# Three input norms of a hybrid encoder: their deviations spread over partitions through a row in DRAM instead of on TensorE

## The reference, cut to what matters

```
h = rmsnorm(x, norm_w[layer, 0]);  m = mixer(h);     x = x + rmsnorm(m, norm_w[layer, 1])
h = rmsnorm(x, norm_w[layer, 2]);  f = conv_ffn(h);  x = x + rmsnorm(f, norm_w[layer, 3])
rmsnorm(x, w) = x * rsqrt(mean(x*x, axis=-1) + eps) * w
```

## Time and profile before

| | |
|---|---|
| median of 3 runs | 1341.23 us (1339.83 to 1341.42) |
| the profiled execution, its own time | 1341.43 us |
| span of its trace | 1339.6 us |
| PE busy | 1320.0 us, 99% of the span |
| DVE, ACT, POOL busy | 777.4, 641.8, 621.8 us |
| data moved by DMA | 119.78 MB |

### The profile page before, as it was taken

One profiled execution on the slowest core, in us unless ns is written; L12 is line 12 of the kernel. 1 busy time (PEld: TensorE's weight loads), 2 busy tenths in 40 slices (PEclk: granted clock), 3 DMA queues, 4 the chain that ended last, 5 costly groups with the idle time before them and its releaser, 6 DMA issues.

```text
span 1339.6 us, 16496 instructions
## 1 busy us (share of the span) xinstructions
PE 1320.0 (99%) x6630; PEld 1119.0 (84%) x6630; DVE 777.4 (58%) x890; ACT 641.8 (48%) x1033; POOL 621.8 (46%) x294
## 2 busy tenths in 40 slices
PE   7999999999999999999999999999999999999997
PEld 6878878888898888888889888898998888888887
DVE  5857386840079998885002753386279988882002
ACT  5654787653355444443233576454554544443221
POOL 3344561245424644445553364554535544445551
PEclk9999999999999999999999999999999999999999
DMA  6332111123223332333333223301323333333331
GB/s 206 95 113 85 51 37 40 63 79 98 92 85 103 97 95 94 94 93 100 94 94 103 96 79 95 95 16 63 112 95 95 95 94 98 102 93 88 100 87 63
DMA packets 41452, 119.78 MB, mean 89 GB/s; under 512 B 4384, under 2 KB 12960, under 8 KB 41376
## 3 DMA queue, kind: packets, MB, share of 16 engines
q1 hardware_dynamic: 40160, 116.34, 28.5%
q10 hardware_dynamic: 1216, 2.38, 0.6%
HBM read 116.35 MB, written 2.23 MB: 89 GB/s over the span
## 4 chain that ended last, share of the span: by engine, by line
PE 93%; DVE 4%; ACT 1%; issue 1%; DMA 0%; ACTq 0%; DVEq 0%
PE bank L336 26%; PE bank L337 26%; PE bank L338 26%; PE bank L1774 1%; PE bank L1775 1%; PE bank L1773 1%; PE bank L2077 1%; PE bank L2059 1%; PE bank L1506 1%; PE bank L1509 1%; PE bank L1325 1%; PE bank L387 1%; PE bank L1292 1%; PE bank L1536 1%; DVE sqacc L663 1%
## 5 line engine op out<-in xcount | busy, mean ns | idle before, releaser
L319 POOL TENSOR_TENSOR wlo<-raw,whi 128x1024 fp32r<-128x1024 f32 (+2 forms) x215 | 531.1, 2483 | 633.9 <-ACT whi L313 633.8
L336 PE MATMUL bank<-xw_hi,whi 128*128 128x512 f32 (+1 forms) x1280 | 478.0, 373 | 8.6 <-DVE xw_lo L646 8.1
L338 PE MATMUL bank<-xw_hi,wlo 128*128 128x512 f32 (+1 forms) x1280 | 473.8, 370 | 0.0
L337 PE MATMUL bank<-xw_lo,whi 128*128 128x512 f32 (+1 forms) x1280 | 473.7, 370 | 0.0
L313 ACT ACTIVATE whi<-raw 128x1024 fp32r<-128x1024 f32 (+2 forms) x217 | 221.5, 1025 | 208.0 <-DMA raw<-in_fout 112.2
L336 PEld LDWEIGHTS bank<-xw_hi,whi 128*128 128x128 f32 x1280 | 242.5, 189 | 50.3 <-issue 8.9
L338 PEld LDWEIGHTS bank<-xw_hi,wlo 128*128 128x128 f32 x1280 | 242.3, 189 | 41.1
L337 PEld LDWEIGHTS bank<-xw_lo,whi 128*128 128x128 f32 x1280 | 242.5, 189 | 39.8 <-issue 0.2
L596 DVE RECIPROCAL small<-small 128x2 f32<-128x2 f32 x8 | 1.3, 165 | 315.1 <-ACT small L521 313.7
L715 DVE SCALAR_TENSOR_TENSOR cbuf<-ubuf,par,cbuf 128x510 f32<-128x510 f32 x100 | 168.7, 1687 | 3.5
L711 DVE SCALAR_TENSOR_TENSOR cbuf<-ubuf,par,cbuf 128x510 f32<-128x510 f32 x100 | 144.6, 1446 | 4.7 <-ACT cbuf L844 4.1
(11 more groups left out here) (278 smaller groups left out, 1453.9 us busy)
## 6 DMA issues: line engine op xcount, KB each, us to landing
raw<-in_fin SPq DMA_DIRECT2D x88, 512.0 KB, 3.6
raw<-in_fout SPq DMA_DIRECT2D x32, 448.0 KB, 3.3
raw<-in_gin SPq DMA_DIRECT2D x25, 512.0 KB, 3.6
raw<-in_hin SPq DMA_DIRECT2D x24, 512.0 KB, 3.7
raw<-in_hout SPq DMA_DIRECT2D x16, 512.0 KB, 3.6
raw<-in_fout SPq DMA_DIRECT2D x16, 512.0 KB, 3.6
raw<-in_gout SPq DMA_DIRECT2D x8, 512.0 KB, 3.9
xres<-in_x SPq DMA_DIRECT2D x8, 256.0 KB, 5.8
```

Source lines behind the costliest of these rows:

```text
L319: engine.tensor_tensor(wlo[s][:, 0:n], raw[s][:, 0:n], whi[s][:, 0:n].bitcast(F32), ALU.subtract).then_inc(w_lo, 1)
L336: first = nc.tensor.matmul(out_ap, wh, ah, start=start, stop=False)
L337: nc.tensor.matmul(out_ap, wh, al, start=False, stop=False)
L338: return first, nc.tensor.matmul(out_ap, wl, ah, start=False, stop=stop)
```

## The change

For norms k = 0, 1 and 2, `pe_res_spread` is no longer called. ACT waits for DVE's reciprocal and issues a DMA that stores `small[:, 12:16]` to a row of 512 values in DRAM (token order, so the 512 values are 4 bytes each, apart from each other on the side of DRAM or of SBUF); it then does the weight splits that it did before, waits until the store has landed, and issues a second DMA that loads this row on all 128 partitions of `rstd`. DVE waits for that load. Norm k = -1 stays as it was.

In `gin`, bank 6 is no longer taken by the spread. Blocks 5 and 6 (and every second later pair, 17 and 18 and so on) swap banks 5 and 6, and the waits that name evictions are renumbered.

Semaphores are merged: the three loads for the GLA stage share one, for which DVE waits ahead of the gate weights; `cst` and `rope` share one, for which every reader of `cst` waits; so do the eight stores of the output, and two steps of POOL at the end.

```diff
+        rstd_row = nc.dram_tensor("rstd_row", (1, T), F32).ap()
         def act_res_rstd(act, k, at):
             act.wait_ge(sem("res_ss"), of("res_ss", k) + 1)
             nc.scalar.activation(small[:, 12:16], bank[7][:, 4:8], ACT.Sqrt, bias=prm("eps"),
                                  scale=1.0 / D).then_inc(sem("res_sd"), 1)
+            if k >= 0:
+                act.wait_ge(sem("res_rs"), of("res_rs", k) + 1)
+                act.dma_start(rstd_row[0].rearrange("(b p) -> p b", p=P), small[:, 12:16],
+                              allow_slow_non_contiguous=True).then_inc(sem("rstd_out"), 16)
             his(act, at)
             if k in (0, 2):
                 his(act, at + 1)
+            if k >= 0:
+                act.wait_ge(sem("rstd_out"), 16 * (k + 1))
+                act.dma_start(rstd[:], rstd_row.broadcast_to([P, T])).then_inc(sem("rstd_in"), 16)
+                return
             act.wait_ge(sem("res_sp"), of("res_sp", k) + 1)
             nc.scalar.activation(rstd[:], bank[6][:], ACT.Copy).then_inc(sem("res_rstd"), 1)
...
         def dve_gate_weights(dve):
-            dve.wait_ge(sem("wgk_in"), 16)
+            dve.wait_ge(sem("gla_in"), 48)
...
-            dve.wait_ge(sem("res_rstd"), of("res_rstd", k) + 1)
+            if k < 0:
+                dve.wait_ge(sem("res_rstd"), 1)
+            else:
+                dve.wait_ge(sem("rstd_in"), 16 * (k + 1))
...
         def pe_fin(pe, l):
-                        beside={2: lambda: pe_res_sums(pe, k), 7: lambda: pe_res_spread(pe, k)} if j == g else None)
+                        beside={2: lambda: pe_res_sums(pe, k)} if j == g else None)
...
         def gbank(j):
-            return bank[(2, 3, 5)[j] if j < 3 else (0, 1, 5, 6)[(j - 3) % 4]]
+            return bank[(2, 3, 5)[j] if j < 3 else (0, 1, 6, 5)[(j - 3) % 4]]
...
         def pe_gin(pe):
                 elif j >= V0 + KD:
-                    pe.wait_ge(sem("vtok_dve" if (j - V0) % 2 else "vtok_act"), (j - V0 - KD) // 2 + 2)
+                    pe.wait_ge(sem("vtok_dve" if j in (V0 + KD, V0 + KD + 3) else "vtok_act"), (j - V0 - KD) // 2 + 2)
                 elif j >= 5:
-                    pe.wait_ge(sem("gin_u"), {5: 3, 6: 1}.get(j, j - 3))
+                    pe.wait_ge(sem("gin_u"), {5: 1, 6: 3}.get(j, j - 3))
                 product(pe, base + j, gbank(j)[:], xw_hi, xw_lo,
-                        beside={6: lambda: pe_res_sums(pe, 1), 8: lambda: pe_res_spread(pe, 1)} if j == 3 else None)
+                        beside={6: lambda: pe_res_sums(pe, 1)} if j == 3 else None)
...
                     if i == 0 and g == 0 and b >= 2:
-                        pe.wait_ge(sem("gin_u"), 4 + b)
+                        pe.wait_ge(sem("gin_u"), 9 - b)
...
-            dve.wait_ge(sem("gmask_in"), 16)
-            dve.wait_ge(sem("tri_in"), 16)
...
-            sp.wait_ge(sem("out_stored"), (NREQ * PAIRS - 1) * 16)
-            sp.wait_ge(sem("last_stored"), 16)
+            sp.wait_ge(sem("out_stored"), NREQ * PAIRS * 16)
```

More of the change, by code:

```diff
@@ L819, in pe_hin @@
                     pe.wait_ge(sem("ident_in"), 16)
-                    pe.wait_ge(sem("cst_in"), 16)
+                    pe.wait_ge(sem("cst_in"), 32)
                 block(j)
@@ L921, in dve_hin @@
             turns(dve, SIDE, Z0, conv)
-            dve.wait_ge(sem("cst_in"), 16)
+            dve.wait_ge(sem("cst_in"), 32)
             dve.wait_ge(sem("ident_in"), 16)
@@ L1054, in act_picks @@
             act.wait_ge(sem("ident_in"), 16)
-            act.wait_ge(sem("cst_in"), 16)
+            act.wait_ge(sem("cst_in"), 32)
             for h in (slice(0, 64), slice(64, 128)):
@@ L1397, in dve_mla_rotated @@
         def dve_mla_rotated(dve):
-            dve.wait_ge(sem("rope_in"), 16)
             dve.wait_ge(sem("mla_kr"), 1)
@@ L1790, in act_gla_loads @@
             act.wait_ge(sem("out_m"), of("out_m", 2))
-            act.dma_start(wgk[:], w_gk).then_inc(sem("wgk_in"), 16)
-            act.dma_start(gmask[:], glac[:, 0:T + CH]).then_inc(sem("gmask_in"), 16)
-            act.dma_start(tri[:], glac[:, T + CH:T + CH + 2 * P]).then_inc(sem("tri_in"), 16)
+            act.dma_start(wgk[:], w_gk).then_inc(sem("gla_in"), 16)
+            act.dma_start(gmask[:], glac[:, 0:T + CH]).then_inc(sem("gla_in"), 16)
+            act.dma_start(tri[:], glac[:, T + CH:T + CH + 2 * P]).then_inc(sem("gla_in"), 16)
         def act_gin(act):
@@ L2331, in _ @@
             act.dma_start(cst[:], consts[:, P:NCONST]).then_inc(sem("cst_in"), 16)
-            act.dma_start(cosin[:], rope).then_inc(sem("rope_in"), 16)
+            act.dma_start(cosin[:], rope).then_inc(sem("cst_in"), 16)
             act_hin(act)
@@ L2348, in _ @@
             nc.scalar.activation(rstd[:, 0:SEQ], bank[5][:, 0:SEQ], ACT.Copy).then_inc(sem("last_rstd"), 1)
-            act.wait_ge(sem("last_x"), 1)
-            act.dma_start(ckr(out, KD - 2, 1, 2), ckr(xres, KD - 2, 1, 2)).then_inc(sem("last_stored"), 16)
+            act.wait_ge(sem("last_x"), 2)
+            act.dma_start(ckr(out, KD - 2, 1, 2), ckr(xres, KD - 2, 1, 2)).then_inc(sem("out_stored"), 16)
         @block.gpsimd
@@ L2369, in _ @@
             nc.gpsimd.tensor_tensor(m, m, rstd[:, 0:SEQ].unsqueeze(1).broadcast_to([P, 2, SEQ]), ALU.mult).then_inc(
-                sem("last_t"), 1)
-            pool.wait_ge(sem("last_t"), 1)
+                sem("last_x"), 1)
+            pool.wait_ge(sem("last_x"), 1)
             nc.gpsimd.tensor_tensor(x, x, m, ALU.add).then_inc(sem("last_x"), 1)
```

## The result

The changed kernel takes 1368.64 us (median of 4 runs, 1367.40 to 1370.35) against 1341.33 us (4 runs, 1339.83 to 1341.78): the ratio is 1.0206, 95% interval 1.0193 to 1.0219. It is 27.3 us slower. The forecast was 1341.9 us, and its range ended at 1346.5.

What follows compares the result with a forecast made beforehand. PE's list was taken to bound the kernel: -2.43 us (three spreads) + 3.1 (wait at gate(0)) + 0 + 0 = +0.7 us, giving 1341.9 us against the median of 1341.23; range 1339.0 to 1346.5.

Steps and rivals of the forecast that it cites:

- PE's list: On PE, three spreads of 0.81 us each leave its work: -2.43 us.
- The two thresholds: PE waits at block 6 of the FFNs from C = 8.4 us on (none expected), at gate(0) C - 3.77 (3.1 us).
- C: Time from the end of DVE's reciprocal through store and load to DVE's start: 6.85 us for k = 1, 8.05 for others.
- The store: ACT's DMA of 512 4-byte pieces to DRAM: 4.0 us for k = 1, 4.6 for others, bounds 2.2 and 7.1.
- The rival of the slow store: Store of 4-byte pieces takes 7.1 us, PE waits at gate(0) and both FFNs: +8.1 us, 1349.3; 1 in 4.
- The load: DMA of the row onto 128 partitions: 2.7 us for k = 1, 3.3 for k = 0 and 2.
- The clock: Rival: PE's clock falls in the wait at gate(0), costing 2.4 us more, 1344.3 in all; 1 in 12.
- ACT's list at nothing: On ACT, three copies go and two issues per norm come; only work needing rstd stands behind the store's wait: no cost.
- The swap: In gin, swapping banks 5 and 6 spares block 5 about 1 us of wait behind a late gate(0).
- the merged semaphores: Waits for GLA loads, cst with rope, and those at the end, on shared semaphores cost nothing; GLA loads have 17 us of cover.

Runs made afterwards that it cites:

- e2: Changed kernel storing only 256 pieces of 4 bytes, the load reading each value for two tokens; 1374.57 us (1 run).
- e3: Changed kernel with its 512 pieces of 4 bytes stored 512 bytes apart in DRAM, the load taking a row of cosines; 1343.10 us (1 run).
- e5: Changed kernel plus unused filler matmuls, 26 ahead of block 6 in each FFN and 38 ahead of gate(0); 1368.29 us, ratio 1.0206 to the kernel before.
- e10: Changed kernel plus unused filler matmuls, 34 ahead of block 6 in each FFN and 42 ahead of gate(0); 1365.8 us (1 run).
- e1: Changed kernel storing 128 pieces of 16 bytes in partition order, DVE reading rstd with a 16-byte step; 1350.11 us, ratio 1.0070 to the kernel before.
- e9: Changed kernel with its 512 pieces of 4 bytes stored 64 bytes apart in DRAM, the load taking a row of cosines; 1342.15 us (1 run).
- e12: e9 with ACT making the weight split of step 4 one turn earlier in both FFNs; 1339.75 us, ratio 0.9996 to the kernel before.
- e7: Changed kernel with the swap of banks 5 and 6 in gin undone; 1371.25 us, ratio 1.0229 to the kernel before.
- e11: Changed kernel without the store, the load taking a row of cosines right after the reciprocal; 1337.59 us, ratio 0.9976 to the kernel before.
- e6: Changed kernel with the load (of cosines) issued right behind the store, without waiting for it to land; 1359.29 us, ratio 1.0138 to the kernel before.
- e4: Changed kernel storing its 512 pieces to a stepped tile in SBUF, small grown by 8 columns, the load taking cosines; 1360.07 us (1 run).

## Why the prediction was wrong, step by step

**PE's list.** Right: 24 matmuls fewer, and 0.90 us a spread in place of 0.81.

**The two thresholds.** Right. PE should wait C - 8.4 us in the FFNs; with the measured C that is 6.66 and 8.09, and PE waited 6.64 and 8.06. At `gate(0)` it should be C - 3.77 = 10.18; it was 9.51, because DVE's steps to `lr_r` took 1.87 us (780.00 to 781.87) against 2.55. The difference is the cast to `lr_r`, 0.43 us against 1.11; before, a step of POOL ran beside it, now POOL was idle, but that this is the reason isn't shown.

**The store.** This is the step that failed. The sum took 4.0 and 4.6 us, with 7.1 as the upper bound; the store took 10.1 to 11.6. Two rows misled. `gt` took 4.6 us amid weight loads, but it was of another kind: 128 KB, not 512 single elements. And 0.15 us a packet of 2.9 KB on queue 1 was taken as the most that a piece of 4 bytes could cost. It was no bound, because no engine's time for a piece is what counts: at k = 1 the pieces had left the engines within 0.6 us, and what followed hung on how densely they lie in DRAM, 8.3 us there beside the same pieces far apart (10.1 against 1.8). The sentence of the Trainium skill on single elements ("DMA: Bandwidth & Descriptors", "Rules for kernel authors"), which I had set beside the sum, pointed the right way, but not to the reason: 512 single elements 64 bytes apart are cheap. The rival of the slow store was right in the term and in the three places, by luck in part: it counted 32 pieces on each engine, behind loads that fill the engines, and neither alone was the cause (e2; and e3, with the same pieces amid the same loads, was cheap). Its end was too low: by its own working, C of 13.95 to 16.49 gives -2.4 + 10.2 + 6.7 + 8.1 = +22.6 us.

**The load.** 3.7, 4.6 and 4.8 us against 2.7 and 3.3, within the bounds of 2.6 and 4.8: mis-sized by 1.0 to 1.5 us a place.

**The clock.** A rival at 8 in 100, for the one wait of 3.1 us. With waits of 6.8 to 9.7 us it came at all three places and cost 6.2 us, on top of the slow store. The two were priced as separate cases, but the second follows from the first. e5 and e10 show that it is the idle time. Its argument against, that the wait is short, doesn't hold: e5 had 8 slow matmuls behind a wait of 1.8 us, and e1 had some behind one of its two waits of 2.5 us, none behind the other.

**ACT's list at nothing.** Wrong, and hidden in the changed kernel by the larger waits. The argument was that behind the wait for the store stands only work that needs `rstd` anyway. That work holds up in turn the split for block 9, which needs no `rstd` but stands further down on the same list. It costs 2.2 us in e9, 2.9 in e3 and 5.0 in e1; e12 takes it away.

**The swap, the merged semaphores.** Right: the swap saves 0.65 us at block 5 (e7), where the forecast said about 1, and no wait for the merged semaphores appears; e11, which has them all, is faster than before.

## What to carry to other kernels

The price of this small store hung on how its pieces lie in DRAM, not on its bytes: before scattering single elements densely into a small row there, make pieces of 16 bytes or keep the elements 64 bytes apart, the two forms that were cheap here. A bound for an operation that the trace doesn't show has to come from rows of its kind; a mean over large packets bounds nothing small. And when a wait enters PE's list, price with it the matmuls that run behind it at the lower clock, and every independent job further down the lists of the engines that wait.

## What the runs showed of the hardware that was not expected

- 512 writes of 4 bytes into 2 KB of DRAM took 10.1 to 11.6 us (9.3 to 11.4 in e5, e7 and e10), the same 64 bytes apart 1.8 to 4.2, though at k = 1 the pieces had left the DMA engines within 0.6 us in both cases; in the meantime the DMA engines showed a share of 0.71 and moved 23 GB/s, and a load of 512 KB took 12.1 us.
- A load right behind such a store, without any wait, landed with it: 9.7 to 11.3 us (e6).
- Reading `rstd` with a step of 16 bytes took DVE 1066 ns in place of 685 (e1). The Trainium skill ("SBUF — State Buffer", "Door 1: The DMA port swizzle (why `[64,N]` ≈ `[32,N]`)") says that SBUF has lines of 16 bytes and that going to a new line on each element has a price; these numbers agree, though no run varied the step.
- With every tile behind `small` moved by 32 bytes (e4), matmuls started 0.233 us apart in place of 0.227, at a granted clock of 0.998. The cause stays open.
